# A transformer block on one core: products with the high half of the weights ahead of those with the low half

## The reference

```
xn = rms_norm(h, norm_mix_g)
proj = xn @ w_in                       # 2048 x 8448: q, k, v of two mixers, two gates
o_a = mixer_a(q_a, k_a, v_a, ...)      # windowed attention with a sink
o_b = mixer_b(q_b, k_b, v_b, ...)      # chunked attention with a relative bias
merged = sigmoid(g_a) * (o_a @ w_branch_a) + sigmoid(g_b) * (o_b @ w_branch_b)
h = h + merged @ w_out
hn = rms_norm(h, norm_ffn_g)
h = h + (silu(hn @ w_ffn_gate) * (hn @ w_ffn_up)) @ w_ffn_down    # 5632 hidden columns
```

## Time and profile before

| | |
|---|---|
| Time, median of 3 runs | 1284.26 us (1283.98 to 1284.26) |
| Profiled execution | 1284.2 us, span 1282.4 us |
| TensorE busy | 1276.3 us (100%), 5961 instructions |
| weight loads busy (PEld) | 1051.1 us (82%) |
| VectorE busy | 991.4 us (77%) |
| ScalarE busy | 732.2 us (57%) |
| GpSimd busy | 79.7 us (6%) |
| Read from HBM | 249.38 MB, 201 GB/s over the span |

### The profile page before, as it was taken

One profiled execution on the slowest core, in us unless ns is written; L12 is line 12 of the kernel. 1 busy time (PEld: TensorE's weight loads), 2 busy tenths in 40 slices (PEclk: granted clock), 3 DMA queues, 4 the chain that ended last, 5 costly groups with the idle time before them and its releaser, 6 DMA issues.

```text
span 1282.4 us, 15314 instructions
## 1 busy us (share of the span) xinstructions
PE 1276.3 (100%) x5961; PEld 1051.1 (82%) x5961; DVE 991.4 (77%) x917; ACT 732.2 (57%) x771; POOL 79.7 (6%) x68
## 2 busy tenths in 40 slices
PE   9999999999999999999999999999999999999999
PEld 7888887777788888888888888888888888888887
DVE  5888777777454565577989988778798888788996
ACT  5776566666444434455656655655565555565653
POOL 1212230000000000000100000000000001000000
PEclk9999999999999999999999999999999999999999
DMA  7876746444565555575876678877867588866874
GB/s 248 304 237 194 234 138 221 153 152 151 212 214 182 180 195 197 189 278 175 276 232 242 186 227 258 258 243 211 277 213 243 182 264 272 252 218 195 282 218 123
DMA packets 137154, 279.68 MB, mean 218 GB/s; under 512 B 5296, under 2 KB 13808, under 8 KB 134272
## 3 DMA queue, kind: packets, MB, share of 16 engines
q1 hardware_dynamic: 130624, 250.37, 55.9%
q0 software_dynamic: 6464, 28.41, 11.9%
HBM read 249.38 MB, written 8.41 MB: 201 GB/s over the span
## 4 chain that ended last, share of the span: by engine, by line
PE 99%; ACT 1%; DVE 0%; issue 0%; POOL 0%; POOLq 0%; ACTq 0%; DVEq 0%
PE bank L1917 22%; PE bank L1919 22%; PE bank L1918 22%; PE bank L1866 10%; PE bank L1868 9%; PE bank L1867 9%; PE bank L1812 1%; PE bank L1839 1%; PE bank L2017 1%; PE bank L1824 1%; PE bank L1797 0%; PE bank L1779 0%; PE bank L1787 0%; PE bank L1772 0%; ACT prob L1003 0%; PE bank L1841 0%
## 5 line engine op out<-in xcount | busy, mean ns | idle before, releaser
L1505 DVE TENSOR_TENSOR u_lo<-quad,u_hi 128x2048 fp32r<-128x2048 f32 x217 | 492.8, 2287 | 97.6 <-PE bank L1919 49.1
L1057 ACT ACTIVATE u_hi<-quad 128x2048 fp32r<-128x2048 f32 x217 | 412.7, 1915 | 258.9 <-PE bank L1919 155.0
L1285 DVE TENSOR_TENSOR w_lo<-raw,w_hi 128x1024 fp32r<-128x1024 f32 (+1 forms) x136 | 162.0, 1193 | 142.3 <-ACT w_hi L904 140.1
L1919 PE MATMUL bank<-u_lo,xT_hi 128*128 128x512 f32 x648 | 252.2, 389 | 0.0
L904 ACT ACTIVATE w_hi<-raw 128x1024 fp32r<-128x1024 f32 (+1 forms) x136 | 140.1, 1034 | 186.7 <-PE bank L1868 177.3
L1917 PE MATMUL bank<-u_hi,xT_hi 128*128 128x512 f32 x612 | 238.6, 390 | 0.3 <-DVE u_lo L1505 0.3
L1918 PE MATMUL bank<-u_hi,xT_lo 128*128 128x512 f32 x612 | 238.1, 389 | 0.0
L1919 PEld LDWEIGHTS bank<-u_lo,xT_hi 128*128 128x128 f32 x648 | 121.6, 188 | 25.3
L1917 PEld LDWEIGHTS bank<-u_hi,xT_hi 128*128 128x128 f32 x612 | 114.9, 188 | 25.1 <-DVE u_lo L1505 1.2
L1918 PEld LDWEIGHTS bank<-u_hi,xT_lo 128*128 128x128 f32 x612 | 114.9, 188 | 23.6
L1866 PE MATMUL bank<-w_hi,xT_hi 128*128 128x512 f32 (+1 forms) x320 | 125.8, 393 | 0.5 <-issue 0.5
(11 more groups left out here) (202 smaller groups left out, 1729.6 us busy)
## 6 DMA issues: line engine op xcount, KB each, us to landing
quad<-in_w_ffn_gate SPq DMA_DIRECT2D x44, 1024.0 KB, 7.2
quad<-in_w_ffn_up SPq DMA_DIRECT2D x44, 1024.0 KB, 5.6
quad<-in_w_ffn_down SPq DMA_DIRECT2D x44, 1024.0 KB, 6.6
raw<-in_w_in SPq DMA_DIRECT2D x32, 1024.0 KB, 5.5
quad<-in_w_in SPq DMA_DIRECT2D x28, 1024.0 KB, 7.5
quad<-quad POOLq DMA_DIRECT2D x20, 1024.0 KB, 8.3
raw<-in_w_out SPq DMA_DIRECT2D x12, 1024.0 KB, 5.0
raw<-in_w_branch_a SPq DMA_DIRECT2D x8, 1024.0 KB, 5.0
```

What stands on the lines that cost most here:

```text
L1057: A(st.hi[u.hi][:], st.quad[slot][:], ACT.Copy).then_inc(hi_ready, u.step)
L1285: V.tensor_tensor(w_lo[:, p % SPLIT_SLOTS, 0:w], raw[:, (j.chunk0 + k // 2) % RAW_SLOTS, (k % 2) * w:(k % 2 + 1) * w], w_hi[:, p % SPLIT_S ...
L1505: V.tensor_tensor(st.lo[u.lo][:], st.quad[u.panel.slot[u.raw]][:], st.hi[u.hi][:].bitcast(F32), ALU.subtract).then_inc(lo_ready, u.step)
L1919: ins = M(sums, a_hi(k), lo[:, w], start=False, stop=k == UNIT_KT - 1, skip_group_check=True)
```

## The change

Only TensorE's list changes. In each piece and each unit, the products with the high half of the weights (x_hi w_hi and x_lo w_hi) come first, behind a wait for hi_ready alone; then comes the wait for lo_ready, and the products x_hi w_lo. In units over both halves of the tokens (O units and N units) the high products of both halves stand ahead of all low products; in an N unit the wait for e_seeded moves with the bottom half's high products, so that it stands behind 8 products instead of 12, and a_summed and c_summed are signalled behind the 20th product instead of the 12th. The very last unit of the kernel keeps its halves one after the other. The number of products is the same. The diff, shortened:

```diff
             def multiply(j, k):
...
-                pe.wait_ge(lo_ready, p + 1 + j.off)
+                pe.wait_ge(hi_ready, p + 1 + j.off)
...
                     for t in range(T):
                         sums = bank[2 * j.pair + t][:, 0:j.cols]
-                        x_hi, x_lo = hi[:, j.kt0 + kt, tokens(t)], lo[:, j.kt0 + kt, tokens(t)]
-                        M(sums, x_hi, w_hi[:, p % SPLIT_SLOTS, w], start=kt == 0, stop=False)
-                        M(sums, x_lo, w_hi[:, p % SPLIT_SLOTS, w], start=False, stop=False)
-                        ins = M(sums, x_hi, w_lo[:, p % SPLIT_SLOTS, w], start=False, stop=kt == j.kts - 1)
+                        M(sums, hi[:, j.kt0 + kt, tokens(t)], w_hi[:, p % SPLIT_SLOTS, w], start=kt == 0, stop=False)
+                        M(sums, lo[:, j.kt0 + kt, tokens(t)], w_hi[:, p % SPLIT_SLOTS, w], start=False, stop=False)
+                pe.wait_ge(lo_ready, p + 1 + j.off)
+                for q in range(PIECE_KT):
+                    kt = k * PIECE_KT + q
+                    w = slice(q * j.cols, (q + 1) * j.cols)
+                    for t in range(T):
+                        sums = bank[2 * j.pair + t][:, 0:j.cols]
+                        ins = M(sums, hi[:, j.kt0 + kt, tokens(t)], w_lo[:, p % SPLIT_SLOTS, w], start=False,
+                                stop=kt == j.kts - 1)
                 ins.then_inc(piece_used, 1)
...
+            def high_products(u, dst, a_hi, a_lo, start, col0=0, cols=COLS):
+
+                hi = u.panel.stage.hi[u.hi]
                 for k in range(UNIT_KT):
                     w = slice(k * COLS + col0, k * COLS + col0 + cols)
+                    sums = dst[:, col0:col0 + cols]
                     M(sums, a_hi(k), hi[:, w], start=start and k == 0, stop=False, skip_group_check=True)
                     M(sums, a_lo(k), hi[:, w], start=False, stop=False, skip_group_check=True)
-                    ins = M(sums, a_hi(k), lo[:, w], start=False, stop=k == UNIT_KT - 1, skip_group_check=True)
+
+            def low_products(u, dst, a_hi, col0=0, cols=COLS):
+
+                lo = u.panel.stage.lo[u.lo]
+                for k in range(UNIT_KT):
+                    w = slice(k * COLS + col0, k * COLS + col0 + cols)
+                    ins = M(dst[:, col0:col0 + cols], a_hi(k), lo[:, w], start=False, stop=k == UNIT_KT - 1,
+                            skip_group_check=True)
                 return ins
+
+            def product(u, dst, a_hi, a_lo, start, col0=0, cols=COLS):
+
+                high_products(u, dst, a_hi, a_lo, start, col0, cols)
+                pe.wait_ge(lo_ready, u.index + 1)
+                return low_products(u, dst, a_hi, col0, cols)
...
             def first_v_unit(u):
+                pe.wait_ge(hi_ready, u.index + 1)
+                for t in range(T):
+                    high_products(u, bank[4 + t], *rows_of((xT_hi, xT_lo), u.kt0, t), u.kt0 == 0)
                 pe.wait_ge(lo_ready, u.index + 1)
                 for t in range(T):
-                    ins = product(u, bank[4 + t], *rows_of((xT_hi, xT_lo), u.kt0, t), u.kt0 == 0)
+                    ins = low_products(u, bank[4 + t], rows_of((xT_hi, xT_lo), u.kt0, t)[0])
                 ins.then_inc(piece_used, u.step)
...
             def unit(u):
...
-                pe.wait_ge(lo_ready, u.index + 1)
+                pe.wait_ge(hi_ready, u.index + 1)
...
-                    ins = product(u, top(panel), *own(panel, u.kt0, 0), False)
+                    last = u is panels[-1].order[-1]
+                    high_products(u, top(panel), *own(panel, u.kt0, 0), False)
+                    if not last:
+                        pe.wait_ge(e_seeded, panel.n + 1)
+                        high_products(u, bottom(panel), *own(panel, u.kt0, 1), False)
+                    pe.wait_ge(lo_ready, u.index + 1)
+                    ins = low_products(u, top(panel), own(panel, u.kt0, 0)[0])
                     if u.index == panel.a_done:
                         ins.then_inc(a_summed, 1)
                     if u.index == panel.c_done:
                         ins.then_inc(c_summed, 1)
-                    pe.wait_ge(e_seeded, panel.n + 1)
-                    if u is panels[-1].order[-1]:
+                    if last:
                         half = COLS // 2
+                        pe.wait_ge(e_seeded, panel.n + 1)
...
                     else:
-                        ins = product(u, bottom(panel), *own(panel, u.kt0, 1), False)
+                        ins = low_products(u, bottom(panel), own(panel, u.kt0, 1)[0])
```

More of the change, by code:

```diff
@@ L1909, in do_job @@
                         (values if a % 2 else turn_probs)(a // 2 - 1)
-            def product(u, dst, a_hi, a_lo, start, col0=0, cols=COLS):
-                hi, lo = u.panel.stage.hi[u.hi], u.panel.stage.lo[u.lo]
-                sums = dst[:, col0:col0 + cols]
+            def high_products(u, dst, a_hi, a_lo, start, col0=0, cols=COLS):
+                hi = u.panel.stage.hi[u.hi]
                 for k in range(UNIT_KT):
                     w = slice(k * COLS + col0, k * COLS + col0 + cols)
+                    sums = dst[:, col0:col0 + cols]
                     M(sums, a_hi(k), hi[:, w], start=start and k == 0, stop=False, skip_group_check=True)
                     M(sums, a_lo(k), hi[:, w], start=False, stop=False, skip_group_check=True)
-                    ins = M(sums, a_hi(k), lo[:, w], start=False, stop=k == UNIT_KT - 1, skip_group_check=True)
-                return ins
+            def low_products(u, dst, a_hi, col0=0, cols=COLS):
[4 more added lines that the diff above has]
+                            skip_group_check=True)
+                return ins
+            def product(u, dst, a_hi, a_lo, start, col0=0, cols=COLS):
+                high_products(u, dst, a_hi, a_lo, start, col0, cols)
+                pe.wait_ge(lo_ready, u.index + 1)
+                return low_products(u, dst, a_hi, col0, cols)
             def rows_of(tiles, kt0, t):
@@ L2034, in out_unit @@
                 for t in range(T):
-                    ins = product(u, bank[2 + t], *rows_of((mT_hi, mT_lo), u.kt0, t), u.kt0 == 0)
+                    high_products(u, bank[2 + t], *rows_of((mT_hi, mT_lo), u.kt0, t), u.kt0 == 0)
+                pe.wait_ge(lo_ready, u.index + 1)
+                for t in range(T):
+                    ins = low_products(u, bank[2 + t], rows_of((mT_hi, mT_lo), u.kt0, t)[0])
                 ins.then_inc(piece_used, 1)
```

## The result

The changed kernel takes 1286.57 us (median of 18 runs, 1286.16 to 1287.27), the kernel before 1284.22 us beside it (18 runs, 1283.78 to 1284.41). The ratio is 1.0019, with a 95% interval of 1.0012 to 1.0025: slower by 2.35 us. The forecast was 1285.3 with a range to 1287.0. So the time lies in the range, and 1.3 us above the forecast. All of this stays under the 0.2% (2.6 us) named there; the interval nevertheless excludes a ratio of 1, and the ends of the units in the trace show where the microseconds are.

What follows compares the result with a forecast made beforehand. TensorE was taken as the bound, busy 1276.3 of 1282.4 us, with products 0.227 us apart. The terms gave 1284.2 - 1.5 + 2.4 + 0.1 = 1285.2 us, stated as 1285.3, range 1282.5 to 1287.0.

Steps and rivals of the forecast that it cites:

- Added waits and the order of the banks: One lo_ready wait per piece and unit, and more bank changes in pieces: value 0, upper end 0.5 us for bank changes.
- Rivals 3 and 4: 3: added waits hold up weight loads, 1323 us, chance 0.03; 4: bank changes halve the clock, 1517 us, chance 0.01.
- rival 5: The change does more than seen, removing stalls inside busy time that no interval showed: 1281.5 us, chance 0.03.
- Gains, 1.47: TensorE starts that waited for the low half of a weight block come earlier: 1.47 us in sum, all taken as lasting.
- (b): Third piece, at 15.42, and fifth piece, at 22.03, start earlier: 0.19 us each, 0.38 together.
- (c): Unit O2, at 60.53, no longer starts late nor has a late next product: gain 0.12 + 0.11 = 0.23 us.
- (d): Eighth piece, at 32.41, starts in time but its weight load was late: gain 0.09 us.
- (a): First product, at 8.85, waited for w_lo and would start at 8.08: gain 0.77 us.
- rival 2: Gains of the first 60 us swallowed by weight loads, wait for e_seeded decides: 1286.7 us, chance 0.10.
- Losses at the four N0 units, 2.42: Where seed_e queues behind a split, e_seeded is needed 0.9 us earlier: 0.51 + 0.88 + 0.63 + 0.40 = 2.42 us.
- rival 1: Gain alone, e_seeded costing nothing new at the four N0, plus 0.5 at 167.96: 1282.2 to 1282.8 us, chance 0.18.
- a_summed and c_summed later: Top sums signalled 1.81 us later: hidden in the 11 gate panels, 0.1 us at M1 after the evacuation at 1241.05.

Runs made afterwards that it cites:

- The order experiment: Changed kernel with lo_ready waited for ahead of each piece and unit, and N units half by half: 1284.29 us against 1284.25 for the kernel before.
- the pieces alone: Fourth experiment: the kernel before with the new order and waits only in the pieces (multiply), units as before: 1283.40 us against 1284.31.
- the first experiment: Changed kernel, but every N unit finishes its top half, low products too, before waiting for e_seeded: 1282.94 us against 1284.31 for the kernel before.
- the last experiment: The first experiment's kernel with seed_e moved ahead of the split for M3 in the third heads panel alone: 1282.13 us against 1284.25 for the kernel before.
- the N0 order alone: Kernel before, but in each N0 except the short panel's, e_seeded's wait and the bottom half's high products stand behind 8 products: 1286.63 us against 1284.25.

## Why the prediction was right, and where it was not

**What bounds the kernel, and reading intervals instead of busy time: right.** Every jump but one was at a place that the intervals of the earlier trace rows had named.

**Added waits and the order of the banks, value 0: right.** The order experiment has 0.04 us in the medians, and the offset of the pieces alone stays flat from 340 to 573 us. Rivals 3 and 4 are excluded, and so is the upper end of 0.5 us for bank changes; of rival 5, a gain that no interval showed, there is no trace either.

**Gains, 1.47: right, with 1.44 in this pair of traces.** (b), (c) and (d) were each 0.03 to 0.06 too low in absolute size, since a stall is followed by a few steps of 0.23 to 0.24. (a) came out at 0.57, not 0.77, and not for a reason of the change: from the transposes of the second block of x to the first product it took 8.85 - 7.29 = 1.56 before and 8.28 - 7.48 = 0.80 after, a gain of 0.76, but those transposes began 0.19 later. I had taken the start of a DMA's landing from one execution as fixed. One pair of traces gives (a) only roughly: against the trace of the kernel before, the first piece is 0.05 to 0.80 us early in the seven kernels whose pieces start on the high half. On average their first product starts at 8.33 us, and at 8.95 in the five that wait for the low half, a gain of 0.62. The gains did last to the end, as the first and fourth experiments show, so the mechanism of rival 2 (gains swallowed) is excluded, although its time, 1286.7, is next to the measured one. The time alone would have pointed to the wrong case.

**Losses at the four N0 units, 2.42: right at 2.35.** Three of four were within 0.04. The third heads panel was 0.16 less, because VectorE was ahead by more than TensorE there: seed_e ended 1.00 us earlier than in the earlier trace rows, while TensorE, before this unit, was 0.81 earlier. The 0.5 at which the prediction, in rival 1, put the old stall of this unit was also too small: when it was removed, in the last experiment, 0.73 us went (its 0.51 of interval, 0.10 for the late load behind it, and steps above 0.227). Rival 1 is excluded.

**a_summed and c_summed later: right for the gate panels, wrong in the short one. This is the step that failed.** For a gate panel I asked what stands behind ScalarE's waiting instruction and found 2.09 us of cover over 1.81. Timeline of ScalarE after, the same split:

```profile
666.77 1.92 ACT L1057 ACTIVATE u_hi<-quad 128x2048 fp32r<-128x2048 f32 x1 [0.28 <-PE bank L1931]
```

2.09 - 1.81 = 0.28, and it starts when the unit ends, as before, so nothing was lost in 11 panels. At the evacuation of the earlier trace rows I called the place tight and then asked only who waits for the evacuation itself (M1: 0.1 forecast, 0.14 measured), not what stands behind it on ScalarE. There the next split is not held back by the unit's end. It started at once behind the evacuation, at 1241.55, so it had no cover at all, and VectorE's list behind it had 0.42 us of room in 18 us. The same question asked a second time would have given 1.81 - 0.42 = 1.39 and a sum of 1285.2 + 1.3 = 1286.5, where 1286.57 was measured. The kernels with the N0 order alone and with the signal 9 products late, each the kernel before with one edit, show both large terms separately: 2.34 and, for a somewhat longer delay, 1.62.

**The range** held the time by 0.4 us, but not through the case meant for it: its upper end came from rival 2, whose mechanism did not happen, and nothing in it stood for the missed term. That the time fell inside is luck.

## What to carry to other kernels

When a signal comes later, ask two questions and not one: who waits for the result, and what is queued behind the waiting instruction on its own engine. Follow that queue until it meets idle time larger than the delay; here it took 18 us and three engines, and the second question decided 1.25 of the 3.74 us that were lost. Idle time in that queue counts only if it doesn't move along with the delay itself, as the wait of 1.98 us did. An order that lets work begin earlier on one input (the high half) is worth having only as long as it doesn't also make another input (the seeded bank) due earlier, or another output (the top sum) late. Where traces of single executions are compared, the jumps of unit ends find terms of 0.1 us that the medians of 11 runs can't.

## What the runs showed of the hardware that was not expected

- **Landing of the first loads.** The transposes of the second block of x began between 7.04 and 7.95 us in the twelve executions traced, in kernels that don't differ up to there. Timeline of TensorE in the kernel with halves by turn only in the short panel, and in the kernel with the signal 9 products late:

```profile
7.17 0.66 PE L1772 MATMUL bank<-ident,x_rows 128*128 128x128 f32 x4 [0.38 <-DMA x_rows<-in_x]
```

```profile
7.85 0.66 PE L1772 MATMUL bank<-ident,x_rows 128*128 128x128 f32 x4 [1.04 <-DMA x_rows<-in_x]
```

  Between these two that is 0.7 us of offset from the start on, half of the whole gain of this change. In the last experiment's trace they began at 7.95, against 7.29 before, which is why it ends only 1.56 us early while the median is 2.12 us lower.
- **A wait that is met costs nothing, one that is late costs a little more than its length.** With an added wait in each of the 360 pieces and units the offset between the jumps stays flat to 0.07 us. A late one starts its product 0.05 to 0.06 us after the release, the neighbour comes 0.10 to 0.11 us late, and some steps of 0.23 to 0.24 follow.
- **GpSimd's root over 128x16 values** takes about 5 us from the sums of squares to its end in both traces (129.84 to 135.00 in the kernel with seed_e ahead of the split, 129.32 to 134.51 in the first experiment), scaling included: a link between VectorE's reduction and its next multiplication. Nothing in the prediction had looked at it, and it carried a delay of VectorE from one panel to the next.
